# A two-layer encoder: expert slots spread over partitions, attention scores in three fp32r products ahead of the rest, DFT tables walked once, the head norm inside the next projection

## The reference

```python
def diff_attention(...):            # layer 0, 4 heads, two score maps per head, d_k = 64, d_v = 128
    sc = einsum('bhcqd,bhckd->bhcqk', q_blk, k)      # c = 0, 1
    p = softmax(sc, axis=-1)
    w = p[:, :, 0] - lam * p[:, :, 1]
    o = einsum('bhqk,bhkd->bhqd', w, v)
    ...
    o = rms_norm(o, subln) * (1.0 - lambda_init)     # per head: the "head norm"

def hyena_mixer(...):               # layer 0, 512 channels
    uc = centered_dwconv(u, conv_w, conv_b)          # from the same input projection
    x1, x2, v = split(uc, 3)
    z = v * x2
    y = irfft(rfft(z) * rfft(kern))[:, :length]      # length 1024, transforms of 2048
    return (y + z * skip) * x1

def hier_moe(x, ...):               # both layers: top 1 of 4 groups, then top 2 of 8 experts
    for each expert e of 32: rows = the tokens that chose e
        out[rows] += gate * ((silu(rows @ w1[e]) * (rows @ w3[e])) @ w2[e])
```

## Time and profile before

| | |
|---|---|
| median of 3 runs | 3127.3 us (3124.83 to 3128.31) |
| time of the profiled execution | 3125.78 us |
| its span, first to last instruction | 3123.9 us |
| PE busy | 2656.7 us, 85% |
| DVE busy | 1901.5 us, 61% |
| ACT busy | 1413.1 us, 45% |
| POOL busy | 347.0 us, 11% |
| mean granted clock of PE | 0.923 of full speed |
| read from HBM | 515.65 MB, 183 GB/s over the span |

### The profile page before, as it was taken

One profiled execution on the slowest core, in us unless ns is written; L12 is line 12 of the kernel. 1 busy time (PEld: TensorE's weight loads), 2 busy tenths in 40 slices (PEclk: granted clock), 3 DMA queues, 4 the chain that ended last, 5 costly groups with the idle time before them and its releaser, 6 DMA issues. The chain is left out here.

```text
span 3123.9 us, 34125 instructions
## 1 busy us (share of the span) xinstructions
PE 2656.7 (85%) x12312; PEld 2036.0 (65%) x12312; DVE 1901.5 (61%) x2277; ACT 1413.1 (45%) x1683; POOL 347.0 (11%) x332
## 2 busy tenths in 40 slices
PE   6989979788698599999996799969687699999994
PEld 5755548623256377777775689958564578877772
DVE  5737764432733588888885530029843788888881
ACT  4424451130012277777774421224421477777770
POOL 0000000000000022222221000003200123322210
PEclk9989989879899699999998899979888799999997
DMA  4100000102114199999997110210123499999992
GB/s 149 54 29 1 1 4 27 63 27 67 67 61 166 62 344 350 351 361 355 350 352 275 65 54 28 95 41 1 50 110 127 171 363 374 365 364 359 369 338 90
DMA packets 88976, 537.58 MB, mean 172 GB/s; under 512 B 18759, under 2 KB 24391, under 8 KB 63400
## 3 DMA queue, kind: packets, MB, share of 16 engines
q1 hardware_dynamic: 65544, 498.37, 41.7%
q0 software_dynamic: 18720, 33.61, 4.4%
q10 hardware_dynamic: 4608, 4.20, 0.4%
HBM read 515.65 MB, written 55.05 MB: 183 GB/s over the span
## 5 line engine op out<-in xcount | busy, mean ns | idle before, releaser
L1835 DVE TENSOR_TENSOR wL<-ring,wH 128x2048 fp32r<-128x2048 f32 x384 | 875.7, 2289 | 202.5 <-ACT wH L1782 202.1
L1782 ACT CAST wH<-ring 128x2048 fp32r<-128x2048 f32 x384 | 732.1, 1909 | 353.7 <-DMA ring<-in_moe_w 289.5
L1701 PE MATMUL psum<-wH,xgH 128*128 128x512 f32 x1024 | 413.8, 404 | 59.5 <-DVE xgL L1835 59.1
L1703 PE MATMUL psum<-wH,xgL 128*128 128x512 f32 x1024 | 403.3, 394 | 0.0
L1709 PE MATMUL psum<-wL,xgH 128*128 128x512 f32 x1024 | 276.6, 392 | 0.0
L1701 PEld LDWEIGHTS psum<-wH,xgH 128*128 128x128 f32 x1024 | 194.0, 189 | 118.1 <-issue 65.1
L1709 PEld LDWEIGHTS psum<-wL,xgH 128*128 128x128 f32 x1024 | 193.8, 189 | 42.2
L1703 PEld LDWEIGHTS psum<-wH,xgL 128*128 128x128 f32 x1024 | 194.4, 190 | 38.0
L1701 PE MATMUL psum<-wH,hidH 128*128 128x512 f32 x512 | 207.6, 405 | 10.1 <-DVE hidL L1835 10.1
L1703 PE MATMUL psum<-wH,hidL 128*128 128x512 f32 x512 | 201.6, 394 | 0.0
L190 PE MATMUL psum<-w_high_vo,xn_high 128*128 128x256 f32 x512 | 143.8, 281 | 5.4 <-DVE ring_rest L185 5.4
(11 more groups left out here) (399 smaller groups left out, 4914.6 us busy)
## 6 DMA issues: line engine op xcount, KB each, us to landing
ring<-in_moe_w SPq DMA_DIRECT2D x192, 2048.0 KB, 11.2
ring<-in_ev_w_in SPq DMA_DIRECT2D x6, 2048.0 KB, 12.8
ring<-in_od_w_in SPq DMA_DIRECT2D x6, 2048.0 KB, 9.1
dft_tables<-in_c_dft SPq DMA_DIRECT2D x32, 256.0 KB, 3.0
xn_scratch<-xn_out SPq DMA_DIRECT2D x16, 512.0 KB, 3.6
ow<-in_moe_w SPq DMA_DIRECT2D x3, 2048.0 KB, 12.3
x_all<-in_x SPq DMA_DIRECT2D x4, 1024.0 KB, 8.0
ring<-in_ev_w_out SPq DMA_DIRECT2D x2, 2048.0 KB, 7.7
```

The source lines that it names most:

```text
L1701: nc.tensor.matmul(psum[:, bank, :], xh[:, k, :], w3[0][:, n, cols], start=(half == 0 and n == 0), stop=False)
L1703: nc.tensor.matmul(psum[:, bank, :], xl[:, k, :], w3[0][:, n, cols], start=False, stop=False)
L1782: nc.scalar.copy(half_of(wH, b, e, c, half), raw(e, c, half)).then_inc(w_high, 1)
L1835: return nc.vector.tensor_tensor(out, whole, high.bitcast(F32), ALU.subtract)
```

## The change

- `router`: the constant row `s128` is no longer 0 to 127 but `turn_of_partition`. Rank r then lies on partition 8 * (r mod 16) + g, where g is 0, 4, 2, 6, 1, 5, 3, 7 for r div 16 = 0 to 7.
- `attention_project`: k is kept in a high and a rest part, `kH` and `kL`; the rest is a new subtraction on DVE for each of 8 tiles (`move_rest`), and PE's transposes of later k tiles wait for it (`k_rest`).
- `attention`: q is split for each step on GpSimd (a copy and a subtraction of 128 x 128). Scores are three fp32r products for each half and map, with the maps c = 0 and 1 in turns. PE's order in a step is now: all scores of step i, then in turns the two halves of the transposes of step i - 2 and of the values of step i - 3. DVE no longer copies weights or scales them: `combine` makes p0 + ratio * p1 in one operation of 128 x 1024 and 1/l0 is applied by ACT when it copies the output. ACT copies both halves of the transposed weights. The `lam` difference is made after the fourth row maximum.
- `head_norm` for attention is gone as a phase; the same operations stand inside `hyena_project`, whose PSUM ring shrinks from four to three pairs.
- `hyena_forward`: each table piece is loaded once, in two buffers instead of four, and used for `zT` and then for the filter. ACT copies the filter's results too, to `K`. DVE's product for kt waits for that kt alone. The next phase's even tables are loaded once PE is done.

```diff
+    turn_of_partition = 16 * np.array([0, 4, 2, 6, 1, 5, 3, 7])[np.arange(P) % 8] + np.arange(P) // 8
-        np.arange(NG, 0, -1), np.arange(EG, 0, -1), np.arange(NE), P * np.arange(1, 8), np.arange(P),
+        np.arange(NG, 0, -1), np.arange(EG, 0, -1), np.arange(NE), P * np.arange(1, 8), turn_of_partition,
...
+                            if i >= NT + 2:
+                                pe.wait_ge(k_rest, i - NT - 1)
...
+                        def move_rest(j):
+                            js = slice(j * P, (j + 1) * P)
+                            dve.wait_ge(qk_moved, NT + j + 1)
+                            rest_of(kL[:, :, js], psum[:, 4 + j % 2, :].rearrange("p (h t) -> p h t", h=AH),
+                                    kH[:, :, js]).then_inc(k_rest, 1)
...
+                        def scores(i, half):
                             h, j = divmod(i, NT)
+                            if half == 0:
+                                pe.wait_ge(q_rest, i + 1)
+                                if i >= 1:
+                                    pe.wait_ge(expd, 2 * i - 1)
+                            products = ((qH, kH), (qL, kH), (qH, kL))
+                            keys = slice(half * 512, (half + 1) * 512)
+                            for n, (qs, ks) in enumerate(products):
+                                for c in range(2):
+                                    rows = slice(c * DK, (c + 1) * DK)
+                                    u = 2 * i + c
+                                    last = nc.tensor.matmul(psum[:, 2 * (u % 3) + half, :], qs[rows, i % 2, :],
+                                                            ks[rows, h, keys], start=(n == 0), stop=(n == 2))
+                                    if half == 1 and n == 2:
+                                        last.then_inc(scored, 1)
...
+                        for i in range(STEPS + 3):
                             if i < STEPS:
+                                scores(i, 0)
+                                scores(i, 1)
+                            for half in range(2):
+                                if 0 <= i - 2 < STEPS:
+                                    turn(i - 2, half)
+                                if i >= 3:
+                                    values(i - 3, half)
+
+                    @block.gpsimd
+                    def _(pool_e):
+                        for i in range(STEPS):
...
+                            nc.gpsimd.tensor_copy(qH[:, b, :], piece).then_inc(q_high, 1)
+                            pool_e.wait_ge(q_high, i + 1)
+                            nc.gpsimd.tensor_tensor(qL[:, b, :], piece, qH[:, b, :].bitcast(F32), ALU.subtract
+                                                    ).then_inc(q_rest, 1)
...
-                            n = did(nc.vector.tensor_scalar(pr[:, b, 1, :], pr[:, b, 1, :], r[:, b, 1:2], None, ALU.mult))
...
+                            nc.vector.scalar_tensor_tensor(out=pr[:, b, 1, :], in0=pr[:, b, 1, :], scalar=ratio[:, b:b + 1],
+                                                           in1=pr[:, b, 0, :], op0=ALU.mult, op1=ALU.add
                                                            ).then_inc(comb, 1)
...
                             if i < STEPS:
                                 row_max(2 * i)
+                                row_max(2 * i + 1)
+                            if i == 1:
+                                difference()
+                            if i >= 1:
                                 combine(i - 1)
...
-                            if i >= 4:
-                                pe.wait_ge(padded, i - 3)
+                            if i >= 3:
+                                pe.wait_ge(padded, i - 2)
...
                             last.then_inc(proj, 1)
+                            if i < NT:
+                                turn(i)
...
                         for n in range(PIECES):
                             pe.wait_ge(piece_ins[n % BUFS], 16 * (n // BUFS + 1))
+                            transform(n, order_of(n, 0), zT)
+                            transform(n, order_of(n, 1), hs if n % 4 < 2 else hd)
+                            if n == 2:
+                                transform(n, MID, hs, slice(0, 1))
...
-                            dve.wait_ge(copied, PIECES)
-                            dve.wait_ge(row_moved, 1)
-                            dve.wait_ge(used, PIECES + 4 * kt + 4)
+                            dve.wait_ge(copied, order_of(4 * kt + 3, 1) + 1)
```

More of the change, by code:

```diff
@@ L279, in attention_project @@
         @phase
[L280 removed]
+        def attention_project(q, kH, kL, v):
             (proj, qk_read, squared, summed, mean_ok, root_ok, normed, turned, qk_moved, v_copied, tab_in,
[L283 removed]
+             chain, x_high, x_rest, w_high, w_rest, k_rest) = take(17)
             with ExitStack() as st:
@@ L513, in values @@
                             h, j = divmod(i, NT)
[L514 to L517, removed]
+                            if half == 0:
+                                pe.wait_ge(wt_hi, i + 1)
+                                if i:
+                                    pe.wait_ge(o_copied, i)
+                            for k in range(4 * half, 4 * half + 4):
@@ L518, in values @@
                                 last = nc.tensor.matmul(psum[:, OB, (i % 2) * DV:(i % 2 + 1) * DV], wT[:, i % 2, k, :],
                                                         v[:, k, h * DV:(h + 1) * DV], start=(k == 0), stop=(k == NT - 1))
[L520 to L525, removed]
-                            if i < STEPS:
[L527 to L533, removed]
+                            if half:
+                                last.then_inc(summed, 1)
@@ L893, in hyena_project @@
         @phase
-        def hyena_project(z, yT, xnH):
-            (proj, padded, convolved, weights_in, edges, chain, x_high, x_rest, w_high, w_rest) = take(10)
+        def hyena_project(z, yT, xnH, o, gain, post):
+            (proj, padded, convolved, weights_in, edges, chain, x_high, x_rest, w_high, w_rest,
+             gain_in, squared, mean_ok, root_ok, scaled, turned, copied) = take(17)
             with ExitStack() as st:
+                sq = sb(st, "sq_att", [P, 2, AH * DV])
+                ss, ms, sd, rs = (sb(st, f"{n}_att", [P, NT, AH]) for n in ("ss", "ms", "sd", "rs"))
+                g_bc = sb(st, "g_att", [P, AH * DV])
                 up = sb(st, "u_padded", [P, 2, T + 2])
@@ L962, in _, with mean, scale @@
                         did = Tally(chain)
+                        def mean(j):
+                            dve.wait_ge(squared, j + 1)
+                            nc.vector.tensor_scalar(ms[:, j, :], ss[:, j, :], 1.0 / DV, EPS, ALU.mult, ALU.add
+                                                    ).then_inc(mean_ok, 1)
+                        def scale(j):
+                            dve.wait_ge(root_ok, j + 1)
+                            dve.wait_ge(chain, did(nc.vector.reciprocal(rs[:, j, :], sd[:, j, :])))
+                            for h in range(AH):
+                                ins = nc.vector.scalar_tensor_tensor(out=o[:, j, head(h)], in0=o[:, j, head(h)],
+                                                                     scalar=rs[:, j, h:h + 1], in1=g_bc[:, head(h)],
+                                                                     op0=ALU.mult, op1=ALU.mult)
+                            ins.then_inc(scaled, 1)
                         def split_w(i):
@@ L978, in _ @@
                         dve.wait_ge(weights_in, 32)
+                        dve.wait_ge(gain_in, 16)
+                        dve.wait_ge(chain, did(nc.vector.tensor_scalar(g_bc[:], g_bc[:], post, None, ALU.mult)))
+                        mean(0)
+                        scale(0)
                         for i in range(STEPS):
                             split_w(i + 2)
+                            if i + 1 < NT:
+                                mean(i + 1)
                             c, ct = divmod(i, HC)
```

238 lines of the change are left out of this document (131 added, 107 removed).

## The result

The changed kernel takes 2933.09 us, the median of four runs (2930.73 to 2936.7), against 3127.81 us (four runs too, 3124.83 to 3136.47). The ratio is 0.9378, with a 95% interval of 0.9355 to 0.9401. The profiled execution took 2935.33 us with a span of 2933.5.

What follows compares the result with a forecast made beforehand. PE and DMA were taken as near their limits in the experts, and PE at 91% in attention. From 3125.8 us, -90 + 1 - 15.3 - 18.6 - 35 = -158 gave 2968 us, range 2936 to 3016.

Steps and rivals of the forecast that it cites:

- Experts: -35 forecast: Both expert stages: spreading the filled partitions saves 35 us, chosen between bounds of 0 and -59.
- the bound itself: Experts: PE can give back at most its own listed wait for the gathered rows' rest part, 59.1 us.
- The mechanism: Experts: 64 ranks load half of the 16 DMA engines; after the change four rows fall to each.
- The rival of a turn the wrong way round: Experts: ranks were even before and now load eight engines; 3140 us, slower by 0.4%; chance 0.02.
- no difference: Experts: the slots make no difference, as HBM or the chunk chain sets the rate; 3003 us; chance 0.15.
- Attention: -90 forecast: Attention: steps of 4.6 us in place of 7.17, an earlier start and a 12 us tail save 90 us.
- Pairs: Attention: score products of the two maps run together on different row halves, 6 x 0.23 = 1.4 us a step.
- the rival said 45: Attention: score pairs don't run together in fp32r, so attention gains 45 us; 3013 us; chance 0.12.
- The hand-off rival: Attention: a loop of hand-offs sets the step at 5.3 us, +22 us; 2990 us; chance 0.11.
- The rule of the Trainium skill: Attention: two-SBUF-input DVE and SBUF-reading GpSimd operations exclude each other; DVE's step estimated at 4.5 us, under PE's.
- Head norm: -15.3 forecast: Head norm: its 18.9 us phase goes, 3.6 us of transposes return on PE, the rest moves under PE; -15.3 us.
- Forward transforms: -18.6 forecast: `hyena_forward`: the end moves from 836.3 to 817.7 us as DVE no longer starts after 20 transforms; -18.6 us, surest term.

Runs made afterwards that it cites:

- the run without rows: Kernel before with every expert slot marked empty, so gathers and scatters run but move no row: 3042.84 us, ratio 0.9732.
- the place of ranks 32 to 63: Changed kernel, two other partition orders, ranks 32 to 63 lying 16 or 32 partitions further than ranks 0 to 31: 2946.82 against 3001.19 us.
- the undone run: Changed kernel with the head norm as its own phase again and the projection of before: 2946.89 us, ratio 0.9446.
- the finer turn: Changed kernel with any 16 consecutive ranks in 16 different partition groups: 2939.32 us, against 2932.2 for the changed kernel beside it.
- three and three: Changed kernel with the three score products of map 0 issued before those of map 1: 2934.65 us, ratio 0.9393.
- six and six: Changed kernel with all six score products of map 0 issued before the six of map 1: 2952.99 us, ratio 0.9441.

## Why the prediction was right or wrong

**Experts: -35 forecast, -68.2 measured. This is the step that failed**, in two places. The first is the choice within the bounds. "DMA would fall just below PE's need rather than far below" was a guess: queue q0 costs 80 us in the kernel before (the run without rows), and even sharing takes nearly all of that away. The other is the bound itself. "PE can give back at most its own wait, 59.1 us" takes the idle time in the profile for the whole stall. But 16.1 of the 66.7 us lay inside PE's *busy* time. PE's timeline of the kernel before shows how, at one such stall:

```profile
1400.12 0.49 PE L1701 MATMUL psum<-wH,xgH 128*128 128x512 f32 x1 [0.89 <-DVE xgL L1835]
1400.45 0.39 PE L1703 MATMUL psum<-wH,xgL 128*128 128x512 f32 x1
1400.67 0.39 PE L1701 MATMUL psum<-wH,xgH 128*128 128x512 f32 x1
1400.90 0.40 PE L1703 MATMUL psum<-wH,xgL 128*128 128x512 f32 x1
```

The recorded end of a product stands 0.39 us after its start while the next starts 0.23 us after, so each stall hides 0.16 us; and the first product after the pause is followed after 0.33 us and not 0.23, another 0.10. The 59.1 us are 47 stalls. Counted from the starts in the traces, the windows of before hold 39 more spacings above 0.5 us than those of after (49 against 10) and 39 more of 0.31 to 0.36 (172 against 133): 39 x 0.26 = 10 us. Another 3 us are clock. Twice, behind the two longest of these stalls (2.4 and 2.3 us idle), the granted clock fell to 0.50 (the lower of the two levels, 1.2 GHz) for 3.4 us, and eight products each time took 0.43 us in place of 0.23. After the change the only stretch like that in the windows ends the second window, and before has that one too. The first of the two:

```profile
1575.10:1578.50 3.40, 3.40 (x9) 2.64 (x8) 3.40 (x2) 3.40 (x3) 0.90 (x1) 0.50 0.68 239
```

Some 3 of the 16.1 us are left, a part of them four slower products at the start of the first window.

The mechanism was right as put. The Trainium skill, "DMA: Bandwidth & Descriptors", section "The descriptor swizzle", gives groups of four neighbours, the second group 32 partitions further, and two halves of engines, for one transfer of 1 MiB to all 128 partitions. The runs agree for gathers and scatters with half of the partitions filled: the place of ranks 32 to 63 alone made 54 us, with 1337.0 against 1391.5 us in the stages. The rival of a turn the wrong way round is dead, as the ranks 0 to 63 of the changed kernel lie on even partitions and are fast; so is "no difference".

**Attention: -90 forecast, -91.6 measured.** Pairs: right, 0.23 to 0.24 us a pair, and worth 44 us where the rival said 45. The step is 4.42 us, PE's own 4.4 without the 0.2 I added for hand-offs. Of the 5 us which that saved, some 2 were lost in the first steps, where the row maxima of a step stand 5.5 to 7.3 us behind those of the step before, and 2 in the tail, 14 us from the last scores to the next phase where I had 12. So the match within 2 us is in part luck. The hand-off rival is out: the step's PE rows show no wait. The rule of the Trainium skill, "SBUF — State Buffer", section "SBUF: two separate sides", couldn't be weighed, since in the timeline GpSimd's two operations (0.29 and 0.45 us, under the 0.60 assumed) lie beside the row maxima and not beside the combination, which stayed at 1.28 us.

**`attention_project`** costs 0.2 us where 1 was forecast. Neither value is shown: in the other runs with the changed phase it ends at 187.7 to 190.5 us, and in the two with the old one at 188.3 and 188.4.

**Head norm: -15.3 forecast, -14.9 measured** (-16.4 by the undone run's stages, whose projection took 147.6 us against 146.1 in the kernel before). `hyena_project` is longer by 149.7 - 146.1 = 3.6 us, the eight groups at 0.45.

**Forward transforms: -18.6 forecast, -18.8 measured.** As worked out, PE's last result is copied at 695.44 and DVE's last product sets the end, first and last row of it:

```profile
695.44 0.58 ACT L1338 COPY filter_freq<-psum 128x512 f32<-128x512 f32 x1 [2.85 <-PE psum L1323]
```

```profile
696.11 2.50 DVE L1370 TENSOR_TENSOR freq_acc<-Z,filter_freq 128x512 f32<-128x512 f32 x4 [9.78 <-ACT filter_freq L1338]
...
711.30 2.50 DVE L1390 TENSOR_TENSOR Z<-freq_acc,freq_tmp 128x512 f32<-128x512 f32 x4
```

**`hyena_filter`: nothing forecast, +2.7 measured**, with the same instructions. The change alone doesn't make it: the changed kernel run again, the same program, took 74.4 us in this stage. Over its first 25 us the first profile has a granted clock of 0.50, the second 0.57, as the kernel before has:

```profile
499.00:524.00 25.00, 13.17 (x35) 7.04 (x36) 7.93 (x9) 4.25 (x6) 0.00 (x0) 0.50 0.16 50
```

```profile
499.00:524.00 25.00, 12.69 (x34) 6.78 (x35) 7.82 (x8) 4.25 (x6) 0.00 (x0) 0.57 0.15 51
```

The other profiles, all with the same instructions in this stage, have 74.2 to 77.5 us, and the finer turn 82.1. I count it as scatter between executions. The three profiles in which all of these phases are the old ones have 74.7 or 74.8, so the change may make the long ones more frequent; that and what selects them stay open.

**The sum.** 2968 is 33 us above the profiled 2935.3, and the experts' term alone is 33.2 off. The range failed because its lower end, 2936, was built from the 59 us bound: with the 68.2 that the experts gave, the same sum reaches 2925.

## What to carry to other kernels

Before a bound is put on what a stall can give back, count the stalls and look at the spacing behind them: idle time in a profile of pipelined products is a lower bound for what the stalls cost, here 51 of 67 us. Where rows are gathered or scattered by index with half of the partitions filled, as here, choose the partitions so that the filled ones fall to all DMA engines, and check it with a pair of runs that move one block of ranks; after that, finer evenness bought nothing. Before a stage's small difference is explained, profile the same kernel twice. Products that use half of the rows each run in pairs at no loss if the other half's first product stands three places behind in the order; at six places the pairs came late, for 20 us.

## What the runs showed of the hardware that was not expected

- PE starts a product for one half of the rows while products for the other half, issued earlier, still wait. With three and three issued, all six pair up, at a cost of nothing (2934.65 us); with six and six, the seventh issued starts beside the third, with three waiting ahead, the second map runs 0.58 us behind the first, and the step grows from 4.42 to 4.98 us.
- Two fp32r products of 64 rows and 512 columns on different halves take 0.24 us together, on the same half 0.47 us.
- Whether ranks 32 to 63 lie 16 or 32 partitions further than ranks 0 to 31 changes the expert stages by 54 us at equal bytes and packets.
- A copy and a subtraction of 128 x 128 on GpSimd take 0.29 and 0.45 us, where the earlier trace rows had 0.60 for another operation of that size.
